# Adding the rows of experts 29 and 30 in one pass, a second bank for expert 30's down products, and an earlier place for expert 0's first token tile

## The reference

```python
def hierarchical_moe(h, ...):
    ...
    # each token: the best of 4 groups, then the best 2 of the 8 experts in it, with weights
    ...
    def expert_block(args):
        xb, e = args
        hid = jax.nn.silu(xb @ w_gate[e]) * (xb @ w_up[e])   # 2048 -> 512
        return hid @ w_down[e]                               # 512 -> 2048
    ...
    y = y * row_w[:, None].astype(y.dtype)
    out = jax.ops.segment_sum(y, row_tok, num_segments=T + 1)[:T]
    ...
x = layer_norm(ALPHA * x + moe(x), ln2_scale, ln2_bias)
```

## Time and profile before

| | us |
|---|---|
| median of 3 executions | 2056.97 |
| lowest and highest | 2056.35, 2057.52 |
| the profiled execution, its own time | 2061.3 |
| its span, first to last instruction | 2059.5 |
| mean granted TensorE clock of the span | 0.908 |

### The profile page before, as it was taken

How to read it: one execution, slowest core, us unless ns; L and a number is a source line. 1 busy time by engine, 2 the same in 40 slices (tenths; PEclk the granted TensorE clock), 3 DMA queues, 4 the chain that set the end, 5 groups by cost and what they waited for, 6 DMA issues and landing times.

```text
span 2059.5 us, 25116 instructions
## 1 busy us (share of the span) xinstructions
PE 1783.2 (87%) x9868; PEld 1151.2 (56%) x9868; DVE 995.0 (48%) x1469; ACT 751.4 (36%) x1321; POOL 15.3 (1%) x34
## 2 busy tenths in 40 slices
PE   9999999999999999999999977766776676666677
PEld 7888888888888888888888532211221122112222
DVE  5454454555444444566565555344433443344357
ACT  5444444344444444454453423122222222122221
POOL 0000000000000000000000000000000000000000
PEclk9999999999999999999999978777787777777778
DMA  7556655455556555466677999999999999999998
GB/s 246 193 176 191 197 176 178 148 184 188 190 184 192 171 186 176 154 191 234 221 278 290 378 430 421 429 433 432 431 433 431 432 432 430 433 431 433 431 427 335
DMA packets 131010, 615.07 MB, mean 299 GB/s; under 512 B 13108, under 2 KB 13780, under 8 KB 116720
## 3 DMA queue, kind: packets, MB, share of 16 engines
q1 hardware_dynamic: 130208, 611.74, 77.0%
q0 software_dynamic: 720, 2.18, 0.6%
HBM read 609.61 MB, written 2.36 MB: 297 GB/s over the span
## 4 chain that ended last, share of the span: by engine, by line
PE 60%; DMA 26%; issue 10%; DVE 2%; ACT 1%; DVEq 0%; POOL 0%; POOLq 0%; SPq 0%; ACTq 0%
DMA W<-in_w_expert_up_dram 25%; PE PS L603 14%; PE PS L605 14%; PE PS L604 14%; PE PS L1217 11%; PE PS L1194 2%; PE PS L1150 1%; PE PS L983 1%; PE PS L1259 1%; DVE ZACC L2267 1%; PE PS L1330 0%; DMA VC<-VS 0%; PE PS L1073 0%; PE PS L960 0%; DMA XN<-in_x_dram 0%
## 5 line engine op out<-in xcount | busy, mean ns | idle before, releaser
L580 DVE TENSOR_TENSOR WL<-RAW,WH 128x1024 fp32r<-128x1024 f32 x384 | 457.5, 1222 | 400.4 <-ACT WH L576 399.1
L576 ACT ACTIVATE WH<-RAW 128x1024 fp32r<-128x1024 f32 x384 | 394.6, 1058 | 260.8 <-PE PS L605 198.9
L603 PE MATMUL PS<-WH,XH 128*128 128x512 f32 x1216 | 479.9, 395 | 0.1
L605 PE MATMUL PS<-WH,XL 128*128 128x512 f32 x1216 | 474.0, 390 | 0.0
L604 PE MATMUL PS<-WL,XH 128*128 128x512 f32 x1216 | 473.2, 389 | 0.0
L1217 PE MATMUL PS<-W,XE 128*32 128x512 f32 x1728 | 244.8, 730 | 120.2 <-DMA W<-in_w_expert_up_dram 120.2
L603 PEld LDWEIGHTS PS<-WH,XH 128*128 128x128 f32 x1216 | 228.3, 188 | 49.5 <-issue 1.7
L605 PEld LDWEIGHTS PS<-WH,XL 128*128 128x128 f32 x1216 | 228.2, 188 | 48.6
L604 PEld LDWEIGHTS PS<-WL,XH 128*128 128x128 f32 x1216 | 228.5, 188 | 45.4
L1217 PEld LDWEIGHTS PS<-W,XE 128*32 128x32 f32 x1728 | 62.4, 131 | 321.9 <-issue 210.3
L2218 DVE TENSOR_TENSOR GSUM_H<-PS,GB 32x512 f32<-32x512 f32 x31 | 21.0, 678 | 363.0 <-ACT UB L1671 363.0
(11 more groups left out here) (335 smaller groups left out, 1530.8 us busy)
## 6 DMA issues: line engine op xcount, KB each, us to landing
RAW<-in_w_in_dram SPq DMA_DIRECT2D x304, 512.0 KB, 4.5
W<-in_w_expert_down_dram SPq DMA_DIRECT2D x28, 4096.0 KB, 29.0
W<-in_w_expert_gate_dram SPq DMA_DIRECT2D x27, 4096.0 KB, 34.8
W<-in_w_expert_up_dram SPq DMA_DIRECT2D x27, 4096.0 KB, 19.9
RAW<-in_w_branch_ret_dram SPq DMA_DIRECT2D x32, 512.0 KB, 5.1
RAW<-in_w_out_dram SPq DMA_DIRECT2D x32, 512.0 KB, 5.8
W<-in_w_expert_down_dram SPq DMA_DIRECT2D x7, 2048.0 KB, 28.1
W<-in_w_expert_gate_dram SPq DMA_DIRECT2D x7, 2048.0 KB, 10.9
```

Of the source, the lines that this page charges most:

```text
L576: act.activation(WH[:, i % RING], RAW[:, i % RING], ACT.Copy).then_inc(hi_done, 1)
L580: dve.tensor_tensor(WL[:, i % RING], RAW[:, i % RING], WH[:, i % RING].bitcast(F32), ALU.subtract).then_inc(lo_done, 1)
L603: pe.matmul(PS[:, bank + t], hs, wh, start=first and j == 0, stop=False)
L605: mm = pe.matmul(PS[:, bank + t], ls, wh, start=False, stop=end)
```

## The change

Expert 0's first token tile is spread ahead of `gate_up_whole(3, 3)`, and VectorE makes item 1's row weights between the two additions of item 0. At the end, item 30's down products go to bank 3 from a hidden buffer of their own (HT30), item 29's YH and YL have buffers of their own, and the rows of 29 and 30 are summed in the PSUM banks: sixteen matmuls for each token tile, then one pair of additions where there were two. `turn_hidden(30)` goes ahead of the second half of `down(29)`, VectorE's `hidden(30)` ahead of the second additions of item 28, and `hidden_last` behind all four `norm_rows`. The waits on `added` and `spread` are renumbered to fit.

```diff
+    YH29 = at("YH29", 44, [QC], F32R)
+    YL29 = at("YL29", 46, [QC], F32R)
+    HT30 = at("HT30", 30.5, [KH, ROWS])
...
                 if last and q == 1 and j == 3:
-                    spread_norm2(2)
                     for m in range(2):
                         pe.wait_ge(late_landed[m], 16)
...
-        def down(item, k4, blocks, first=False, halves=False, more=False):
+        def down(item, k4, blocks, first=False, halves=False, more=False, ht=HT, bank=Y_BANK):
...
-                    if not first:
+                    if bank == XE_BANK:
+                        pe.wait_ge(xe_stored, NE * QS)
+                    elif not first:
                         pe.wait_ge(y_dve, item)
...
+        def spread_part(t, m, gs, y, start, stop):
+            rows = slice(m * ROWS, (m + 1) * ROWS)
+            return pe.matmul(PS[:, SPREAD + m], gs[rows, t * P:(t + 1) * P], y[rows, :], start=start, stop=stop)
+        def spread_29():
+            pe.wait_ge(g_ready, NE - 2)
+            pe.wait_ge(added, (NE - 3) * 4 + 2)
+            pe.wait_ge(y_dve, NE - 2)
+            for y in (YH29, YL29):
+                for m in range(QD):
+                    spread_part(0, m, GS29, y, y is YH29, False)
+        def spread_30():
+            pe.wait_ge(g_ready, NE - 1)
+            pe.wait_ge(y_act, NE - 1)
+            for m in range(QD):
+                spread_part(0, m, GS30, YH, False, False)
+            pe.wait_ge(y_dve, NE - 1)
+            for m in range(QD):
+                mm = spread_part(0, m, GS30, YL, False, True)
+                if m % 2:
+                    mm.then_inc(spread, 2)
+        def spread_both(n):
+            pe.wait_ge(added, (NE - 3) * 4 + 4 + 2 * n)
+            for gs, y in ((GS29, YH29), (GS29, YL29), (GS30, YH), (GS30, YL)):
+                for m in range(2 * n, 2 * n + 2):
+                    mm = spread_part(1, m, gs, y, y is YH29, y is YL)
+            mm.then_inc(spread, 2)
...
+        spread_rows(0, 0)
         pe.wait_ge(h_ready, 3)
         gate_up_whole(3, 3)
-        for t in range(TOK):
-            spread_rows(0, t)
+        spread_rows(0, 1)
         turn_hidden(2)
...
         spread_rows(NE - 4, 1)
+        turn_hidden(NE - 2)
         down(NE - 3, 1, (2, 3), halves=True)
-        pe.wait_ge(h_ready, NE - 1)
-        turn_hidden(NE - 2)
-        spread_rows(NE - 3, 0, GS29, by_pairs=True)
-        down(NE - 2, 2, (0, 1), halves=True)
-        spread_rows(NE - 3, 1, GS29, by_pairs=True)
-        down(NE - 2, 2, (2, 3), halves=True)
-        pe.wait_ge(xe_stored, NE * QS)
-        keep_busy(XE_BANK, 1, rid, Z[:, 0, 0:CH])
-        for t in range(TOK):
-            spread_rows(NE - 2, t, GS30, by_pairs=True)
-            if t == 0:
-                keep_busy(XE_BANK, 2, rid, Z[:, 0, 0:CH])
+        down(NE - 2, 2, range(KH), halves=True, ht=HT30, bank=XE_BANK)
+        spread_29()
+        keep_busy(GU_BANK, 1, rid, Z[:, 0, 0:CH])
+        spread_30()
+        keep_busy(GU_BANK, 1, rid, Z[:, 0, 0:CH])
+        for n in range(2):
+            spread_both(n)
         number_slots()
         spread_compact(0)
-        spread_norm2(0)
+        for j in range(2):
+            spread_norm2(j)
         gate_up(NE - 1, 3, 0, take(1), last=True)
-        spread_norm2(1)
         spread_compact(1)
         gather_sums()
+        for j in range(2, 4):
+            spread_norm2(j)
         gate_up(NE - 1, 3, 1, take(1), last=True)
-        spread_norm2(3)
...
+        rows_scaled(NE - 1, 1, range(1))
         hidden_tanh(NE - 2)
-        rows_scaled(NE - 1, 1)
-        y_high(NE - 3, W29)
-        hidden_copy(NE - 2)
-        y_high(NE - 2, W30)
+        rows_scaled(NE - 1, 1, range(1, QS))
+        hidden_copy(NE - 2, HT30)
...
+        act.activation(YH29[:], PS[:, Y_BANK], ACT.Copy, scale=W29[:, 0:1]).then_inc(y_act, 1)
...
+        act.activation(YH[:], PS[:, XE_BANK], ACT.Copy, scale=W30[:, 0:1]).then_inc(y_act, 1)
...
+        def add_both(t):
+            for n in range(2):
+                dve.wait_ge(spread, (NE - 3) * 4 + 4 * t + 2 * n + 2)
+                z = ZACC[:, t, n * 2 * QC:(n + 1) * 2 * QC].rearrange("p (m c) -> p m c", m=2)
+                dve.tensor_tensor(z, PS[:, SPREAD + 2 * n:SPREAD + 2 * n + 2], z, ALU.add).then_inc(added, 2)
...
-        for t in range(TOK):
-            add_rows(0, t)
+        add_rows(0, 0)
         row_weights(1)
+        add_rows(0, 1)
         row_tokens(1)
...
         y_low(NE - 4)
-        add_rows(NE - 4, 0)
         row_weights(NE - 2, W30)
         row_tokens(NE - 2, GS30)
+        add_rows(NE - 4, 0)
...
         dve.tensor_scalar(WHALF[:], WROW[:], 0.5, None, ALU.mult)
+        hidden(NE - 2)
+        add_rows(NE - 4, 1)
...
-        hidden(NE - 2)
-        add_rows(NE - 4, 1)
-        y_low(NE - 3, W29)
+        y_low(NE - 3, W29, high=YH29, low=YL29)
+        y_low(NE - 2, W30, bank=XE_BANK)
         for t in range(TOK):
-            add_rows(NE - 3, t)
-        y_low(NE - 2, W30)
-        for t in range(TOK):
-            add_rows(NE - 2, t)
+            add_both(t)
...
-        for j in range(2):
+        for j in range(4):
             norm_rows(j, 0)
-        centre_rows(2, 0)
         hidden_last()
-        scale_rows(2, 0)
-        norm_rows(3, 0)
```

More of the change, by code:

```diff
@@ L1258, in down @@
                     col = (b % KB2) * D + m * QC
-                    mm = pe.matmul(PS[m * ROWS:(m + 1) * ROWS, Y_BANK], HT[:, b],
+                    mm = pe.matmul(PS[m * ROWS:(m + 1) * ROWS, bank], ht[:, b],
                                    W[pair_q][:, b // KB2, col:col + QC], start=b == 0, stop=b == KH - 1)
@@ L1315, in join_stats, with spread_rows @@
                       start=True, stop=True).then_inc(joined, 1)
-        def spread_rows(item, t, gs=GS, by_pairs=False):
+        def spread_rows(item, t):
             if t == 0:
@@ L1320, in spread_rows @@
                 pe.wait_ge(y_act, item + 1)
-            if not by_pairs:
-                pe.wait_ge(added, item * 4 + 2 * t + 2)
+            pe.wait_ge(added, item * 4 + 2 * t + 2)
             for part, y in ((0, YH), (1, YL)):
@@ L1326, in spread_rows @@
                 for m in range(QD):
-                    if by_pairs and part == 0 and m % 2 == 0:
-                        pe.wait_ge(added, item * 4 + 2 * t + 1 + m // 2)
                     rows = slice(m * ROWS, (m + 1) * ROWS)
-                    mm = pe.matmul(PS[:, SPREAD + m], gs[rows, t * P:(t + 1) * P], y[rows, :],
+                    mm = pe.matmul(PS[:, SPREAD + m], GS[rows, t * P:(t + 1) * P], y[rows, :],
                                    start=part == 0, stop=part == 1)
@@ L1357, in spread_norm2 @@
                 pe.wait_ge(ln2_low, 1)
-            if j < 2:
-                pe.wait_ge(added, (NE - 1 + run) * 4 + 1 + j)
+            if j < 2 and run:
+                pe.wait_ge(added, NE * 4 + 1 + j)
+            elif j < 2:
+                pe.wait_ge(added, (NE - 1) * 4 + 2 * j)
             if j >= 2:
@@ L1679, in rows_copy, with rows_scaled @@
             act.activation(xg(item)[:], PS[:, xe_bank(item)], ACT.Copy).then_inc(xg_stored, 1)
-        def rows_scaled(item, buf):
+        def rows_scaled(item, buf, parts=range(QS)):
             first = isinstance(item, int) and item < 2
             act.wait_ge(xe_turned, item + 1)
-            for j in range(QS):
+            for j in parts:
                 for k in range(KQ):
@@ L1693, in rows_scaled, with hidden_copy, y_high @@
                 last.then_inc(xe_stored, 1)
-        def hidden_copy(item):
+        def hidden_copy(item, ht=HT):
             act.wait_ge(h_turned, item + 1)
-            act.activation(HT[:].rearrange("p b n -> p (b n)"), PS[:, HT_BANK, 0:KH * ROWS],
+            act.activation(ht[:].rearrange("p b n -> p (b n)"), PS[:, HT_BANK, 0:KH * ROWS],
                            ACT.Copy).then_inc(ht_ready, 1)
-        def y_high(item, w=WROW):
+        def y_high(item):
             act.wait_ge(d_used, (item + 2) * (UNITS - GU))
@@ L1729, in _ @@
         odd_copy(NE - 2)
+        rows_scaled(NE - 1, 1, range(1))
         hidden_tanh(NE - 2)
-        rows_scaled(NE - 1, 1)
-        y_high(NE - 3, W29)
-        hidden_copy(NE - 2)
-        y_high(NE - 2, W30)
+        rows_scaled(NE - 1, 1, range(1, QS))
+        hidden_copy(NE - 2, HT30)
+        act.wait_ge(d_used, (NE - 1) * (UNITS - GU))
+        act.wait_ge(w_ready, NE - 2)
+        act.activation(YH29[:], PS[:, Y_BANK], ACT.Copy, scale=W29[:, 0:1]).then_inc(y_act, 1)
+        act.wait_ge(d_used, NE * (UNITS - GU))
+        act.wait_ge(w_ready, NE - 1)
+        act.wait_ge(spread, (NE - 3) * 4)
+        act.activation(YH[:], PS[:, XE_BANK], ACT.Copy, scale=W30[:, 0:1]).then_inc(y_act, 1)
         for v in range(2):
@@ L2256, in row_tokens, with y_low @@
             dve.tensor_tensor(gs[:], HIT[:, 0], HIT[:, 1], ALU.add).then_inc(g_ready, 1)
-        def y_low(item, w=WROW):
+        def y_low(item, w=WROW, bank=Y_BANK, high=YH, low=YL):
             dve.wait_ge(y_act, item + 1)
```

(2 more changed lines are left out.)

2 lines of the change are left out of this document (1 added, 1 removed).

## The result

The changed kernel took 2061.97 us (median of 10 executions, 2060.18 to 2064.58); the kernel before, on the same chip, 2057.94 (10 executions, 2056.35 to 2060.11). The ratio is 1.0018 (95% interval 1.0010 to 1.0026): slower by 4.0 us, where -0.7 was predicted. The profiled execution took 2061.89, its span 2059.8.

The account below looks back on a forecast made before the run. Bound: a full stream of weight loads at 431 GB/s, then a chain through VectorE at the end. -1.6 (stream) - 0.2 (to last addition) + 1.1 (to hidden rows) = -0.7 us: 2056.97 to 2056.3, range 2053.9 to 2059.4.

Parts of the forecast that it names:

- every later landing moves 1.6 us earlier: Weight stream after item 5's up load: the closed gap carries through to the end, as the stream is full from there.
- The bound of 1251: Start: latest issue of item 5's up load, were item 4's products at half clock throughout (9.39 us instead of 7.04).
- the -1.6 of the sum: First term, the stream: closing the gap at item 5's up load gains 1.6 us; bounds 0 to 1.8.
- `turn_hidden(30)` and item 30's down products: End: turns finish near 2007.4 under a weight wait; products wait for weights alone, ending at 2020.55, 0.3 us earlier.
- A: End of VectorE's last addition; forecast 2028.15 against 2028.31, in times of before, the stream's 1.6 us not yet subtracted.
- the 1.8 of the sum: At the end of the last addition: the stream's -1.6 and the second term's -0.2 us together.
- the -0.2 of the second term: Up to the last addition, through item 30's down products and the row sums: -0.2 us, bounds -2.1 and +2.3.
- From the last addition to item 31's hidden rows ... +1.1: VectorE at the end: 17.0 us without idle, two whole norm blocks ahead, against 15.86 before.
- H: End of item 31's hidden rows on VectorE; forecast to have these rows some 17 us behind the last addition.
- Nothing behind the hidden rows changes: Kernel's end: no change except an earlier store of the output's second half, for which nothing was taken.
- The rival that ended slower: Half clock from item 30's second half on: +1.8 (2058.8), with item 31's second products too +4.0 (2061.0); chance 0.17.
- the forecast's own signs: Signs of wrong: last addition over 3 us earlier or over 1 later, item 31's second products half-clocked, VectorE idle between blocks.

Follow-up runs that it names:

- start alone: Kernel before with only the change at the start of the mixture; ratio 0.9998 (0.9989 to 1.0007), mean -0.44 us.
- norm order back: Changed kernel with the order of the norm blocks put back as before; ratio 0.9997 (0.9988 to 1.0006), mean -0.54 us.
- with slots early: Changed kernel, old norm order put back, slot matmuls moved between the halves of `down(30)`; ratio 0.9997, mean -1.00 us.
- norm order alone: Kernel before with only the new order of the norm blocks, run twice; ratio 1.0024 both times, means +4.75 and +5.33 us.
- the same with fillers: four: Kernel before with the new norm order and four fillers instead of two ahead of TensorE's last turn; ratio 1.0015, mean +3.49 us.
- and one more: Kernel before with new norm order, four fillers, and another filler between `spread_norm2(2)` and `spread_norm2(3)`; ratio 1.0025, mean +4.89 us.
- the changed kernel's second comparison: The changed kernel, unchanged, measured again on another chip against the kernel before; ratio 1.0013 (1.0004 to 1.0022), mean +2.38 us.
- the unused read: Changed kernel plus a 1 MB read after item 31's down products: 1.0019, mean +3.20 us; with four fillers too: 1.0007, mean +1.77 us.

## Why the prediction was wrong

**The start was right; "every later landing moves 1.6 us earlier" was not.** The gap closed, and the up load was issued within 1.1 us of the forecast. (The bound of 1251 was too early: of the 9.39 us of the earlier trace rows only the part until 1212 was at half clock, granted 0.51, and the rest at 1.00, and by the 3.55 for sixteen matmuls the 64 take 14.2, so that at half clock throughout the load would have been issued near 1255.8. The products ran in 7.04.) From item 4's gate matrix to item 6's, issue plus time to landing, it is 59.7 us in the mean of eight traces with the old start and 58.4 in eight with the new: -1.3. But from item 4's gate matrix to the first half of item 31's, it is 793.40 to 795.18 with the old start (eight traces, mean 794.09) and 792.97 to 793.55 with the new (twelve, mean 793.40): -0.7 for the -1.6 of the sum. About half is lost on the way. In seven of those eight traces with the new start, against two of the eight with the old, some load between items 8 and 29 lands 10.2 to 11.4 us behind the one before it instead of 9.7: the stream, taken to be full from there on, is not. Why is open. Alone the new start gave a mean of -0.44: within an interval of 1.9 a gain of this size can be neither shown nor denied.

**`turn_hidden(30)` and item 30's down products: right in kind.** The turns started at 2004.19, under a wait for weights. The second half took 3.08, between the 1.92 and the 3.55 that I weighed, and ended at 2017.59 where the sum had 2020.55 - 1.6 = 2018.95. (In eight of the ten traces with this order it took 1.92, and the first half 3.2 to 3.6 instead.) The pairs took 2022.94 - 2021.81 = 1.13 for eight matmuls, at full clock, against 0.67 for the fours of the earlier trace rows. The Trainium skill, TensorE: Matmul & The Clock Gate, section Part 3: Packing small matmuls, has it that matmuls in different row groups overlap; with half as many groups 1.13 agrees in direction, though it is 1.7 times and not the double that I worked out from it. From that product's end to A it took 7.91 where I had 7.6. So A came 2.8 us earlier, one more than the 1.8 of the sum; over three profiled executions of each kernel the mean of A is 2.7 earlier. A varies, though: in the eight traces whose code ahead of A is that of the kernel before it lies between 2023.96 and 2028.41 (mean 2026.78), in the ten with the changed code between 2023.64 and 2025.50 (mean 2024.70), which is 2.1 earlier. By these means, with -0.7 for the stream, -1.4 is left for the -0.2 of the second term: that A comes out near the 1.8 of the sum is in part luck, a term too large beside one too small.

**"From the last addition to item 31's hidden rows ... +1.1" failed, in two ways.** VectorE is not without idle: `spread_norm2(2)` stands behind the first products and the gather, and VectorE waits 0.92 for it: 17.74 instead of 17.0. And the 15.86 that I set against it was not the old order's time but one of several. There the hidden rows begin 8.82 us (8.81 to 8.84 in six traces) behind the end of item 31's first products, and this end moves with the time that they take, 5.33 to 6.38 us, and with their start, 0.1 to 1.3 us behind A. The kernel before, in another execution:

```profile
2028.51 5.34 PE L1194 MATMUL PS<-W,XE 128*32 128x512 f32 x32
```

```profile
2026.05 2.36 DVE L2267 TENSOR_TENSOR ZACC<-PS,ZACC 128x1024 f32<-128x1024 f32 x2 [0.62 <-PE PS L1330]
...
2040.15 1.41 DVE L2286 SCALAR_TENSOR_TENSOR OB<-ZACC,MV,PS 128x512 f32<-128x512 f32 x2 [0.51 <-PE PS L1365]
2042.66 0.68 DVE L2231 TENSOR_TENSOR GSUM_H<-PS,GB 32x512 f32<-32x512 f32 x1 [1.10 <-ACT GB L1739]
```

Those products, 6.38 in the earlier trace rows, take 5.34 here, and the idle of 2.12 in the earlier trace rows is 0.51: 2042.66 - 2028.41 = 14.25. In the terms of A and H:

| trace | first products' end behind A | H behind A | item 31's down products | span's end behind H |
|---|---|---|---|---|
| before, three traces | 7.03, 5.44, 7.03 | 18.73, 17.11, 18.71 | 3.64 in all | 12.46, 12.38, 12.39 |
| start alone | 5.43 | 17.12 | 3.64 | 12.39 |
| norm order back; with slots early | 7.46; 5.44 | 19.17; 17.13 | 3.64 | 12.45; 12.42 |
| changed, three traces | 8.33, 8.28, 8.29 | 20.61, 20.54, 20.56 | 3.64 in all | 13.69, 12.92, 12.41 |
| norm order alone, twice | 8.08, 6.46 | 20.34, 22.89 | 6.58, 5.34 | 16.59, 14.90 |
| the same with fillers: four; and one more | 8.11; 6.45 | 20.38; 19.61 | 3.64 | 13.67; 13.19 |

The new order puts one and a half normed blocks (the scaling of block 2, and block 3), which had run under the last down products, ahead of H on the engine that now sets the pace: 19.6 at the least in these traces, where the old order does with 17.1 when TensorE's products end early. Between the three traces of each kernel the term is +1.8 to +3.5 and, by their means, 20.57 - 18.18 = +2.4, not +1.1.

**"Nothing behind the hidden rows changes" failed too.** Of the old order seven traces have 12.4 behind H; the changed kernel has 13.0 in the mean of three. The write of the last rows took 2.7 in all seven; in the changed kernel the second store is issued some 8 us earlier, the queues rest ahead of that write, and it took 4.0, 3.3 and 2.7. And TensorE, which went from the last filler to the last turn with 0.57 us of idle in the old order, stands for 2.15, and then the down products are at half clock in some executions, in four of the profiles with the new norm order and none of the old.

**Where that leaves the sum.** By the means of three traces of each: A -2.7, A to H +2.4, the end +0.6: +0.3 in the span (2058.57 against 2058.30). With the -2.1 of all traces for A it is +0.9. So in the traces the gain ahead of A is there, and the norm order gives it back; the timed executions of the changed kernel with the norm order put back (-0.54) are too few to show that gain. The timed executions of the changed kernel lost more, 4.0 in the first comparison and a mean of 2.4 in the second, so that some 1.5 to 3 us have no place in the traces. Three traces of each are a small base: the three profiled executions of before took 2060.1 us in the mean, where its timed ones have means of 2058.0 to 2059.0. The half clock behind TensorE's waits would give such a difference, being in some executions and not in others, but the three profiled executions of the changed kernel have none of it in item 31's second or down products; fillers took 1.3 to 1.8 off the norm order alone in one version and nothing in two others. So this part is argued, not shown, and its cause stays open. That the norm order carries the loss is shown, twice by itself and twice by putting it back (the second time with the slot matmuls early, on the chip of the changed kernel's second comparison: -1.00 beside +2.38). TensorE's move of `spread_norm2(1)` is not the part of it that costs: alone it cost nothing, and undoing it, in the changed kernel, gained nothing. VectorE's order and the later places of `spread_norm2(2)` and `(3)` were not tried apart.

**A choice at the end of the working** made the miss of the time larger, not that of the change: I carried the 4.3 us by which the profiled execution of before was above the median over to the changed kernel. That execution was above every one of the ten timed beside the changed kernel (2060.11 at most); the changed kernel's profiled one, 2061.89, is close to its median. Without that step 2060.6 would have stood beside 2061.97, near it by luck alone. The rival that ended slower had the half clock at item 30's products and item 31's second ones, and its higher price, 2061.0, lay outside the range that I gave. Where half clock was seen, in four traces of other kernels with the new norm order, it was at item 31's down products and in two of them at its second ones, behind waits for VectorE; of the forecast's own signs the idle between the normed blocks stands in the changed kernel's trace, the second products at half clock do not.

## What to carry to other kernels

When work leaves the shadow of a later product to stand ahead of it, the price is not the work's length less some idle of one trace: ask what the old order takes when the other engine is quick, and whether the new one can follow. Read the base of a difference from more than one profiled execution where its length hangs on the clock. A gap that is closed early in a stream is worth at the end only what no later gap takes back: measure it at the last load. And a product's engine that is made to wait for a slower one may pay twice, by the wait and by the matmuls behind it.

## What the runs showed that I had not expected

- The same idle ahead of the same matmuls led to either clock: 2.15 us and then 3.64 in the changed kernel, 2.16 and then 6.58 with the norm order alone. The Trainium skill, TensorE: Matmul & The Clock Gate, section What's actually happening, says that where the clock changes varies from run to run of one kernel; item 31's first products agree, with 6.38 us in one execution of the kernel before and 5.34 in another.
- The last small write (32 rows by their slots) landed in 2.7 us in all ten traces in which other transfers ran until shortly before it, the two with the unused read among them, and in 2.7 to 4.0 in the ten where the queues had rested (over 3 in eight). The Trainium skill, DMA: Bandwidth & Descriptors, section Latency and other measured facts, says that a lighter load on the memory makes the fixed cost smaller; these runs show no such gain, and the longer times only with the lighter load.
